# MLP down products of a fused two-block transformer kernel: seven block products in place of eight for fifteen of sixteen pairs of feature blocks, with block sums on GpSimd

## The reference

```python
h = rms_norm_2(x, norm1_g[l])
...                                         # four attention branches, out projection
h = rms_norm_2(x, norm2_g[l])
x = x + jnp.square(jax.nn.relu(h @ w_up[l])) @ w_down[l]     # 1024 -> 4096 -> 1024
```

## Time and profile before

| | |
|---|---|
| median of three runs | 1469.63 us |
| the profiled execution: its own time, its span | 1473.47 us, 1471.3 us |
| PE / VectorE / ScalarE / GpSimd busy over the span | 90% / 50% / 36% / 3% |
| MLP of layer 0: first up matmul to last add to x | 957.86 to 1135.79 us |
| MLP of layer 1: the same | 1286.28 to 1464.20 us |

### The profile page before, as it was taken

The page is one execution under the profiler, slowest core; times in us unless marked ns, Lnnn a source line. Parts: engine busy times, 40 slices in busy tenths (PEclk is TensorE's granted clock), DMA queues, the critical chain, the costliest instruction groups (busy, mean ns, idle before and its releaser), DMA issues. The chain is left out here.

```text
span 1471.3 us, 21540 instructions
## 1 busy us (share of the span) xinstructions
PE 1321.8 (90%) x9066; PEld 986.1 (67%) x9066; DVE 729.4 (50%) x1126; ACT 526.3 (36%) x894; POOL 49.6 (3%) x46
## 2 busy tenths in 40 slices
PE   5999998866689999986766999999999999999997
PEld 2765774433347667642433968799988978799996
DVE  1744653211157367421122878665555767765554
ACT  3535331000045344200001536653444436644343
POOL 0200000000002000000000110000000110000000
PEclk9999999988899999998888999999999989999999
DMA  9798899999977958999999605456654405455551
GB/s 354 287 326 309 335 404 420 421 421 421 418 268 280 329 186 349 421 421 420 422 420 390 168 2 200 148 156 206 200 174 147 107 14 188 143 172 193 183 198 42
DMA packets 135976, 392.10 MB, mean 266 GB/s; under 512 B 26816, under 2 KB 40128, under 8 KB 111296
## 3 DMA queue, kind: packets, MB, share of 16 engines
q1 hardware_dynamic: 132128, 389.48, 71.0%
q10 hardware_dynamic: 3744, 1.15, 0.3%
HBM read 389.45 MB, written 1.05 MB: 265 GB/s over the span
## 5 line engine op out<-in xcount | busy, mean ns | idle before, releaser
L421 DVE TENSOR_TENSOR spl<-ring,spl 128x2048 fp32r<-128x2048 f32 x65 | 149.0, 2292 | 135.8 <-ACT spl L412 135.8
L545 PEld LDWEIGHTS ps<-hh,spl 128*128 128x128 f32 x1728 | 204.2, 189 | 6.9 <-issue 5.8
L545 PE MATMUL ps<-hh,spl 128*128 128x256 f32 x1728 | 206.2, 281 | 2.8 <-DVE hh L507 2.8
L412 ACT ACTIVATE spl<-ring 128x2048 fp32r<-128x2048 f32 x66 | 126.6, 1919 | 147.3 <-PE ps L545 107.8
L2348 PE MATMUL ps<-spl,ur 128*128 128x512 f32 x768 | 176.7, 389 | 0.0
L1348 PE MATMUL ps<-ring,ar 128*32 128x256 f32 x960 | 108.4, 472 | 64.7 <-DMA spl_as_slots<-in_w_up 29.8
L2348 PEld LDWEIGHTS ps<-spl,ur 128*128 128x128 f32 x768 | 143.2, 188 | 29.2
L935 DVE TENSOR_TENSOR spl<-ring,spl 128x1024 fp32r<-128x1024 f32 (+2 forms) x120 | 138.2, 1175 | 22.2 <-ACT spl L926 21.8
L1348 PE MATMUL ps<-spl_as_slots,ar 128*32 128x256 f32 x736 | 108.9, 484 | 28.4 <-DMA spl_as_slots<-in_w_up 16.9
L926 ACT ACTIVATE spl<-ring 128x1024 fp32r<-128x1024 f32 (+2 forms) x120 | 116.7, 1010 | 45.0 <-PE ps L525 10.7
L525 PE MATMUL ps<-spl,hh 128*128 128x512 f32 x480 | 117.7, 398 | 3.7 <-DVE hh L1048 1.3
(11 more groups left out here) (370 smaller groups left out, 1792.0 us busy)
## 6 DMA issues: line engine op xcount, KB each, us to landing
ring<-in_w_up SPq DMA_DIRECT2D x58, 1024.0 KB, 5.7
spl_as_slots<-in_w_down SPq DMA_DIRECT2D x50, 1024.0 KB, 16.9
ring<-in_w_ada SPq DMA_DIRECT2D x48, 1024.0 KB, 7.6
ring<-in_w_down SPq DMA_DIRECT2D x40, 1024.0 KB, 5.0
ring<-in_w_in SPq DMA_DIRECT2D x34, 1024.0 KB, 7.5
ring<-in_w_gate SPq DMA_DIRECT2D x34, 1024.0 KB, 16.3
spl_as_slots<-in_w_up SPq DMA_DIRECT2D x30, 1024.0 KB, 17.3
ring<-in_w_out SPq DMA_DIRECT2D x16, 1024.0 KB, 7.6
```

The source lines that it names most:

```text
L412: sc.activation(t.hi, t.raw, ACT.Copy).then_inc(s_hi, 2)
L421: v.tensor_tensor(t.lo, t.raw, t.hi, ALU.subtract).then_inc(s_lo, 1)
L545: ins = pe.matmul(ps[:, banks[m // 2], (m % 2) * 256:(m % 2) * 256 + 256], le, ri, start=(kk == 0 and q == 0 and m % 2 == 0), stop=(kk == ...
```

## The change

For a pair of feature blocks f (two blocks of 128) the down product is a 2 x 2 block product: the activations are A11, A12, A21, A22 (row half by feature block, 128 x 128 each), the weights B11, B12, B21, B22 (feature block by column half, 128 x 512 each). The new code computes it in Winograd's form with seven block products for fifteen of the sixteen pairs of a layer:

A11 B11; A12 B21; S4 B22; S1 (B12 - B11); S3 (B22 - B12); S2 T2; A22 (B21 - T2), where T2 = B22 - (B12 - B11), S1 = A21 + A22, S2 = S1 - A11, S3 = A11 - A21, S4 = A12 - S2.

The seven sums are collected in seven PSUM banks over all fifteen pairs and combined once at the end on VectorE. The sixteenth pair is made with eight products, added into the banks that are by then correct for it. Bank 7 holds the up product, after two other banks for the first chunks.

- The loop has 17 steps with chunks of 256 features (one pair), where it had 9 with 512. An up tile now holds all of k for 256 columns. The step order on TensorE is up(c), then the blocks of pair c-2.
- GpSimd (`pool_mlp`) makes the weight sums (one instruction of 1024 elements a partition, two of 512) and the activation sums (four of 128).
- The hi and lo parts of the down weights are made in four groups of 512, 1024, 1024 and 1024 elements (`act_blocks`, `dve_blocks`), where they were one of 2048; those of the activations are 1024 elements a pair, where they were 512. The square is 512 elements a pair, as before.
- A down tile of the ring comes free when the lo parts of the first two groups and both weight sums are written (`sy_free`).
- The end of the stage: one ScalarE copy of bank 0, then on VectorE six scaled adds onto x and two plain adds, then the four scaled adds of the banks to which the last pair went.
- Buffers of the parts lie over the gate tile and the mixer's space, the weight sums in `xn`.

```diff
-            for c in range(9):
-                if c < 8:
-                    for half in range(2):
-                        tile(("up2", l, c, half), [wu[:, 4 * half:4 * half + 4, c * 512:c * 512 + 512]], 4, 512)
-                if c:
-                    for f2 in range(2):
-                        f0 = 4 * (c - 1) + 2 * f2
-                        tile(("down2", l, c - 1, f2), [wd[:, f0:f0 + 2, :]], 2, 1024)
+
+            def up_tile(c):
+                tile(("up2", l, c), [wu[:, :, 256 * c:256 * c + 256]], 8, 256)
+
+            def down_tile(p):
+                tile(("down2", l, p), [wd[:, 2 * p:2 * p + 2, :]], 2, 1024, split=p == 15, pair=15 * l + p if p < 15 else None)
+
+            for c in range(2):
+                up_tile(c)
+            for c in range(2, 18):
+                if c < 16:
+                    up_tile(c)
+                down_tile(c - 2)
...
+        def sy_free(sy, t):
+            if t.pair is None:
+                sy.wait_ge(*slot_free(t))
+            else:
+                sy.wait_ge(s_bl, 4 * t.pair + 2)
+                sy.wait_ge(s_T, 2 * t.pair + 2)
...
-        ml.stg = [carve(11296 + 1024 * q, 1024) for q in range(2)]
+        ml.uT = [[ur[:, 2048 * q + 1024 * z:2048 * q + 1024 * z + 1024].rearrange("p (b n) -> p b n", n=128) for z in range(2)] for q in range(3)]
+        ml.stg = [carve(6144 + 1024 * q, 8, 128) for q in range(2)]
+        A11, A21, A12, A22, S1, S2, S3, S4 = range(8)
+        ml.first = carve(6144, 512)
+        ml.sums = [xn[:, q, :] for q in range(2)]
+        GROUPS = [(A11,), (A12, S4), (S1, S3), (S2, A22)]
+        BANKS = [(0,), (1, 2), (3, 4), (5, 6)]
+        FIRST_COL, ROW2_COL, FIRST_ROW, LAST = 1, 6, 2, 7
+        ml.parts = []
+        for q, (at, of) in enumerate(((8192, wr), (12544, wr), (10496, wr), (0, gr))):
+            w = 512 * len(GROUPS[q])
+            ml.parts.append([of[:, at + w * z:at + w * z + w] for z in range(2)])
+
+        def up_bank(c):
+            return 7 - c if c < 3 else 7
+
+        def blocks_raw(l, p, q):
+            raw = T["down2", l, p].raw
+            return (raw[:, 0:512], raw[:, 1024:2048], ml.sums[0], ml.sums[1])[q]
+
+        def pe_up(pe, g, l, c):
+            t = T["up2", l, c]
+            pe.wait_ge(s_lo, t.m + 1)
+            if c > 2:
+                pe.wait_ge(s_up2, 17 * l + (1 if c == 3 else c))
+            for m in range(2):
+                for k in range(8):
+                    if c == 0 and m == 0 and k % 2 == 0:
+                        pe.wait_ge(*g(s_hT))
+                    pr = parts3([u[:, k, m * 128:(m + 1) * 128] for u in t.parts], [u[:, k, :] for u in hT])
+                    for q, (le, ri) in enumerate(pr):
+                        ins = pe.matmul(ps[:, up_bank(c), 256 * m:256 * m + 256], le, ri, start=(k == 0 and q == 0 and m == 0), stop=(k == 7 and q == 2),
+                                        skip_group_check=True)
+            ins.then_inc(s_used, 1)
+
+        def pe_blocks(pe, l, p):
+            w = 15 * l + p
+            pe.wait_ge(s_u1, 16 * l + p + 1)
+            if p == 0:
+                pe.wait_ge(s_up2, 17 * l + 3)
+            for q in range(4):
+                pe.wait_ge(s_bl, 4 * w + q + 1)
+                n = len(GROUPS[q])
+                for j in range(n):
+                    pr = parts3([u[:, GROUPS[q][j], :] for u in ml.uT[p % 3]], [u[:, 512 * j:512 * j + 512] for u in ml.parts[q]])
+                    for z, (le, ri) in enumerate(pr):
+                        ins = pe.matmul(ps[:, BANKS[q][j], :], le, ri, start=(p == 0 and z == 0), stop=(p == 14 and z == 2), skip_group_check=True)
+                ins.then_inc(s_bu, 1)
...
         def pe_mlp(pe, g, l):
             pe_x_T(pe, 5 + 2 * l)
-            for c in range(9):
-                if c < 8:
+            for c in range(17):
+                if c < 16:
+                    pe_up(pe, g, l, c)
+                if c > 1:
+                    pe_blocks(pe, l, c - 2)
+            t = T["down2", l, 15]
+            pe.wait_ge(s_lo, t.m + 1)
+            pe.wait_ge(s_u1, 16 * l + 16)
+            for n, bank in enumerate((FIRST_COL, ROW2_COL, FIRST_ROW, LAST)):
+                c, i = divmod(n, 2)
+                for f in range(2):
+                    pr = parts3([u[:, 2 * f + i, :] for u in ml.uT[0]], [u[:, f, c * 512:(c + 1) * 512] for u in t.parts])
+                    for q, (le, ri) in enumerate(pr):
+                        ins = pe.matmul(ps[:, bank, :], le, ri, start=(bank == LAST and f == 0 and q == 0), stop=(f == 1 and q == 2), skip_group_check=True)
+                ins.then_inc(s_col if n < 3 else s_used, 1)
...
+        def act_blocks(sc, l, p, q):
+            w = 15 * l + p
+            if q < 2:
+                t = T["down2", l, p]
+                sc.wait_ge(s_w[t.slot], t.landed)
+            else:
+                sc.wait_ge(s_T, 2 * w + q - 1)
+            if p:
+                sc.wait_ge(s_bu, 4 * (w - 1) + q + 1)
+            sc.activation(ml.parts[q][0], blocks_raw(l, p, q), ACT.Copy).then_inc(s_bh, 1)
+
+        def act_acts(sc, l, p):
+            n = 8 if p < 15 else 4
+            if p < 15:
+                sc.wait_ge(s_S, 15 * l + p + 1)
+            else:
+                sc.wait_ge(s_sqr, 16 * l + 16)
+            if p > 2:
+                sc.wait_ge(s_bu, 4 * (15 * l + p - 2))
+            sc.activation(ml.uT[p % 3][0][:, 0:n, :], ml.stg[p % 2][:, 0:n, :], ACT.Copy).then_inc(s_u0, 1)
+
+        def act_mlp(sc, g, l):
+            last = T["down2", l, 15]
+            act_hT(sc, g, PR(f"n2{l}"), last, 1)
+            for c in range(17):
+                if c > 1:
+                    act_blocks(sc, l, c - 2, 2)
+                    act_blocks(sc, l, c - 2, 3)
+                if c < 16:
+                    sc.wait_ge(s_used, T["up2", l, c].m + 1)
                     if c > 1:
-                        pe.wait_ge(s_up2, 8 * l + c - 1)
-                    run(pe_colsT(pe, g, ("up2", l, c), [4 + 2 * (c % 2), 5 + 2 * (c % 2)], fresh=(c == 0)))
+                        sc.wait_ge(s_u1, 16 * l + c - 1)
+                    sc.activation(ml.stg[c % 2][:, 0:4, :], ps[:, up_bank(c), :].rearrange("p (b n) -> p b n", n=128), ACT.Relu).then_inc(s_up2, 1)
                 if c:
-                    d = c - 1
-                    uv = [u.rearrange("p (f n) -> p f n", f=4) for u in ml.uT[d % 3]]
-                    pe.wait_ge(s_u1, 8 * l + d + 1)
-                    for f2 in range(2):
-                        t = T["down2", l, d, f2]
-                        pe.wait_ge(s_lo, t.m + 1)
-                        for cc in range(2):
-                            for i in range(2):
-                                for f in range(2):
-                                    pr = parts3([u[:, 2 * f2 + f, i * 128:(i + 1) * 128] for u in uv], [u[:, f, cc * 512:(cc + 1) * 512] for u in t.parts])
-                                    for q, (le, ri) in enumerate(pr):
-                                        ins = pe.matmul(ps[:, 2 * cc + i, :], le, ri, start=(d == 0 and f2 == 0 and f == 0 and q == 0),
-                                                        stop=(d == 7 and f2 == 1 and f == 1 and q == 2), skip_group_check=True)
-                                if d == 7 and f2 == 1 and 2 * cc + i < 3:
-                                    ins.then_inc(s_col, 1)
-                        ins.then_inc(s_used, 1)
-
-        def act_mlp(sc, g, l):
-            last = T["down2", l, 7, 1]
-            act_hT(sc, g, PR(f"n2{l}"), last, 1)
-            for c in range(9):
-                if c < 8:
-                    act_hi(sc, last, 2)
-                    sc.wait_ge(s_used, T["up2", l, c, 1].m + 1)
-                    if c > 1:
-                        sc.wait_ge(s_u1, 8 * l + c - 1)
-                    u = ml.stg[c % 2]
-                    for m in range(2):
-                        ins = sc.activation(u[:, 512 * m:512 * m + 512], ps[:, 4 + 2 * (c % 2) + m, :], ACT.Relu)
-                    ins.then_inc(s_up2, 1)
-                    sc.wait_ge(s_sqr, 8 * l + c + 1)
-                    if c > 2:
-                        sc.wait_ge(s_used, T["down2", l, c - 3, 1].m + 1)
-                    sc.activation(ml.uT[c % 3][0], u, ACT.Copy).then_inc(s_u0, 1)
+                    act_acts(sc, l, c - 1)
+                    if c < 16:
+                        act_blocks(sc, l, c - 1, 0)
+                        act_blocks(sc, l, c - 1, 1)
                 if c:
-                    act_hi(sc, last, 2)
+                    act_hi(sc, last, 1)
+            sc.wait_ge(s_u1, 16 * l + 15)
+            sc.wait_ge(s_bu, 60 * l + 57)
+            sc.activation(ml.first, ps[:, 0, :], ACT.Copy).then_inc(s_up2, 1)
...
+        def dve_blocks(v, l, p, q):
+            v.wait_ge(s_bh, 4 * (15 * l + p) + q + 1)
+            v.tensor_tensor(ml.parts[q][1], blocks_raw(l, p, q), ml.parts[q][0], ALU.subtract).then_inc(s_bl, 1)
+
+        def dve_acts(v, l, p):
+            n = 8 if p < 15 else 4
```

(98 more changed lines are left out.)

14 lines of the change are left out of this document (4 added, 10 removed).

## The result

The changed kernel takes 1553.09 us (median of four runs, 1550.87 to 1554.09) against 1469.18 us for the kernel before (median of four too): 1.056 times as long, 95% interval 1.0542 to 1.0579. The forecast was 1554 us.

What follows compares the result with a forecast made beforehand. TensorE was taken to bound the kernel before, VectorE and GpSimd in turns after, at 13.55 us a pair. The layers add 43.2 + 40.9 = 84.1 us to the median 1469.6: 1554 us, own range 1538 to 1580 us.

Steps and rivals of the forecast that it cites:

- PE bounds the kernel before, and its saving is real but small: MLPs: TensorE sets the pace; a pair falls from 11.20 to 10.51 us, 20.7 us in two layers.
- rival 1: MLP steps: VectorE and GpSimd run side by side, PE stays the bound; about 10 us faster, 1460 us; chance 0.06.
- VectorE and GpSimd take turns: MLP steps: operations reading SBUF don't share; the second waits, then needs its own time less about 0.12 to 0.2 us.
- The price of the turns: MLP steps: 15.30 us a pair less 1.75 for up to 14 handovers gives 13.55 us, between 13.0 and 15.3.
- strict alternation: MLP steps: with both queues full the turns of VectorE and GpSimd alternate, up to 14 handovers giving back 0.125 us each.
- The written order reaches that pace: One MLP step: hi parts come in time, the order keeps to 13.55 us, PE idles some 2.7 us a step.
- Head, tail, sum: MLP stage: head 22.5 us, tails 11.9 and 9.6; layers 221.1 and 218.8 us for 177.9 each; 84.1 us added.
- Rival 3: MLP steps: whole instructions exclude each other, no overlap, 15.3 us a step; 1601 us; chance 0.10.
- Rivals 1, 2 and 4: Besides the first: about half of GpSimd's time covered, 1512 us (chance 0.06); gaps where nobody has the turn, 1609 us (0.06).
- Rival 5: MLP steps: the granted clock decides from a mean of 0.78 down; 1749 us at 1.2 GHz throughout; chance 0.03.
- Two signs: MLP windows: PE busy about 78%, and VectorE's 1225 ns lo parts lengthened to 2 us and more.

Runs made afterwards that it cites:

- write_only: Changed kernel with GpSimd's MLP additions replaced by memsets of about the same busy time, sums left out: 1457.38 us, 0.9908 times before.
- reads_2: Kernel with the seven sums on VectorE and the square on ScalarE, plus two unused GpSimd additions of 512 elements a pair: 1518.47 us.
- more_products: Changed kernel with the first group's product made three times in every Strassen pair, six more matmuls of 512 columns: 1551.77 us.

## Why the prediction was right

- *PE bounds the kernel before, and its saving is real but small.* Right. write_only shows it: 13 us; rival 1 had 20.7 less what head and tail take, some 10 us. PE's own prices were a little high: 11.20 and 10.51 us a pair, where the steps of the kernel before take 11.10 (22.21 a chunk) and those of write_only 10.44.
- *VectorE and GpSimd take turns.* Right, and shown from four sides: writes in place of reads (no loss), one operand from PSUM (0.45 us a step less), reads without any wait (loss in proportion), the same reads beside a VectorE with room (no loss).
- *The price of the turns.* 15.30 us of records a step less 14 handovers of 0.125 gave 13.55; measured 13.42. With the durations found alone (15.39 us together) it is 0.14 us a handover. The strict alternation that I assumed is in the timeline of this kernel; it is no rule, as reads_2 shows, and the few handovers of the mixers could not tell that it would hold here; that much is luck. The GpSimd durations, extrapolated from 256, 384 and 1024 elements, came to 0.45, 1.28 and 2.39 us; alone they take 0.46, 1.30 and 2.40.
- *The written order reaches that pace.* Nearly. VectorE stood still 0.58 us a step in front of the activations' lo part, for ScalarE, while GpSimd had the turn, so it cost nothing. PE was to stand still some 2.7 us a step; its weight loads waited 2.7 us a step for VectorE's lo parts in 1000 to 1150 us, its matmuls 2.0.
- *Head, tail, sum.* Of the head 22.5 us were forecast and 23.1 measured (981.05 - 957.98), of the tail of layer 0 11.9 and 12.2. Layer 0 was to take 221.1 us and took 219.7, layer 1 was to take 218.8 and took 217.5. The sum said 84.1 us; the medians differ by 83.9. That they agree to 0.2 us is partly luck: in the profiles the two layers add 81.4 us, and the spans differ by 77.8, with 4.7 us in a mixer that I had held fixed.
- *Rival 3, whole instructions without overlap* (1601 us), is out: the ends in the timeline overlap by 0.13 to 0.15 us each. *Rivals 1, 2 and 4* are out with the step. *Rival 5:* the mean clock was 0.97 and 0.96 in the windows, and more_products, with PE at 1.00 there, took the same time, so the clock cost nothing.
- *Two signs were off.* PE was to be busy 78% of the windows and its records cover 86%. Many matmul records are longer here than with PE full (416 and 447 ns on average at 512 columns, about 390 in write_only), so part of that share is waiting and a lower clock; the weight loads fill 73% here and 91% in the kernel before, where PE is full, a ratio of 0.80. And of the four VectorE instructions of 1024 elements a step only two grew to 2 us and more (2309 and 2773 ns); the two behind GpSimd's additions of 128 elements took 1.47 us: their own 1.22 and the 0.46 ahead of them, less the overlaps.

## What to carry to other kernels

An idle GpSimd is not free help for a VectorE whose operations read two SBUF operands: add the time of both engines, take off 0.11 to 0.2 us for each change of hands, and compare with the bound of the stage. If the sum is over it, put the work on VectorE itself, which needed 1.04 ns an element here against 2.16 on GpSimd, or take one operand from PSUM. Before spending on TensorE's share, ask what the last saved matmul would wait for: here 6% off PE needed VectorE, ScalarE and both ends of the stage to be in time as well, and the best complete version only drew level, with VectorE as its bound.
